# Moving one x step a chunk later, and a set of accumulator loads a few products earlier, in the feed-forward of a hybrid decoder layer

## The reference

```python
x = layer_norm(alpha * x + mix, ln1_g, ln1_b)            # x: (2048, 1024)
ff = jnp.square(jax.nn.relu(x @ w_ff1)) @ w_ff2          # w_ff1: (1024, 4096), w_ff2: (4096, 1024)
x = layer_norm(alpha * x + ff, ln2_g, ln2_b)
```

## Time and profile before

| | before |
|---|---|
| median of 3 runs | 2166.41 us |
| lowest, highest | 2164.86, 2171.97 us |
| the profiled execution's own time | 2171.97 us |
| its span, first to last instruction | 2170.3 us |
| TensorE matmul busy | 2082.6 us, 96% |
| VectorE, ScalarE, GpSimd busy | 64%, 46%, 24% |
| mean granted TensorE clock | 0.987 of full speed |
| DMA, mean over the span | 172 GB/s |

### The profile page before, as it was taken

How to read it: one execution, slowest core, us unless ns; L and a number is a source line. 1 busy time by engine, 2 the same in 40 slices (tenths; PEclk the granted TensorE clock), 3 DMA queues, 4 the chain that set the end, 5 groups by cost and what they waited for, 6 DMA issues and landing times.

```text
span 2170.3 us, 28904 instructions
## 1 busy us (share of the span) xinstructions
PE 2082.6 (96%) x11392; PEld 1685.1 (78%) x11392; DVE 1389.6 (64%) x1898; ACT 1006.3 (46%) x1344; POOL 516.7 (24%) x483
## 2 busy tenths in 40 slices
PE   7999999999999999799999999999999999999996
PEld 5677787778777777688888788888788888788884
DVE  3668566756765687656556776666665645954458
ACT  3535454444444445545445654544433333633334
POOL 3002001101110213011000244444684700810004
PEclk9999999999999999899999999999999999999998
DMA  6222333324242514255646778777968665665563
GB/s 196 59 59 88 107 95 121 107 78 143 72 127 59 175 53 134 87 189 196 221 153 218 270 256 285 248 272 271 333 203 284 196 193 187 222 224 194 193 194 136
DMA packets 241063, 374.26 MB, mean 172 GB/s; under 512 B 16368, under 2 KB 117776, under 8 KB 240928
## 3 DMA queue, kind: packets, MB, share of 16 engines
q1 hardware_dynamic: 212096, 272.68, 38.6%
q0 software_dynamic: 28832, 99.74, 13.3%
HBM read 272.74 MB, written 99.61 MB: 172 GB/s over the span
## 4 chain that ended last, share of the span: by engine, by line
PE 51%; DVE 6%; ACT 2%; DMA 2%; issue 1%; POOL 0%; SPq 0%; DVEq 0%; ACTq 0%; POOLq 0%
PE main L68 9%; PE main L70 9%; PE main L69 9%; PE sc L68 6%; PE sc L69 6%; PE sc L70 6%; DVE w_lo L1563 3%; PE aux L70 1%; PE ob L70 1%; PE ob L68 1%; PE aux L68 1%; PE ob L69 1%; PE aux L69 1%; DMA w_b<-in_w_ff_dram 1%; DMA x_piece<-normed_dram 1%
## 5 line engine op out<-in xcount | busy, mean ns | idle before, releaser
L1563 DVE TENSOR_TENSOR w_lo<-w_b,w_hi 128x1024 fp32r<-128x1024 f32 x144 | 217.5, 1513 | 241.5 <-ACT w_hi L1533 241.5
L1563 DVE TENSOR_TENSOR w_lo<-raw,w_hi 128x1024 fp32r<-128x1024 f32 x144 | 205.5, 1430 | 128.6 <-ACT w_hi L1533 128.6
L1533 ACT ACTIVATE w_hi<-raw 128x1024 fp32r<-128x1024 f32 x144 | 152.5, 1060 | 256.7 <-PE main L70 112.6
L1533 ACT ACTIVATE w_hi<-w_b 128x1024 fp32r<-128x1024 f32 x144 | 152.2, 1057 | 176.9 <-PE aux L70 81.3
L1053 DVE TENSOR_TENSOR w_lo<-raw,w_hi 128x1024 fp32r<-128x1024 f32 x116 | 140.9, 1222 | 140.4 <-ACT w_hi L763 139.6
L68 PE MATMUL main<-xT_lo,w_hi 128*128 128x512 f32 (+1 forms) x528 | 217.2, 411 | 1.5 <-DVE xT_lo L1065 1.5
L69 PE MATMUL main<-xT_hi,w_lo 128*128 128x512 f32 (+1 forms) x528 | 205.5, 389 | 0.0
L70 PE MATMUL main<-xT_hi,w_hi 128*128 128x512 f32 (+1 forms) x528 | 205.4, 389 | 0.0
L68 PE MATMUL sc<-x_lo,w_hi 128*128 128x512 f32 x448 | 175.6, 392 | 8.4 <-DVE x_lo L1506 6.1
L68 PE MATMUL main<-x_lo,w_hi 128*128 128x512 f32 x448 | 175.7, 392 | 8.0 <-ACT z L1884 8.0
L68 PE MATMUL main<-w_lo,w_hi 128*128 128x512 f32 x448 | 175.8, 392 | 5.1 <-DVE w_lo L1563 5.0
(11 more groups left out here) (254 smaller groups left out, 4664.7 us busy)
## 6 DMA issues: line engine op xcount, KB each, us to landing
raw<-in_w_in_dram SPq DMA_DIRECT2D x80, 512.0 KB, 3.7
h_dram<-z SPq DMA_DIRECT2D x64, 512.0 KB, 3.9
raw<-h_dram SPq DMA_DIRECT2D x112, 256.0 KB, 2.7
w_b<-h_dram SPq DMA_DIRECT2D x112, 256.0 KB, 2.7
h_dram<-h_s SPq DMA_DIRECT2D x48, 512.0 KB, 4.0
rows<-in_x_dram POOLq DMA_DIRECT2D x32, 512.0 KB, 4.9
raw<-in_w_out_dram SPq DMA_DIRECT2D x32, 512.0 KB, 3.7
raw<-in_w_ff_dram SPq DMA_DIRECT2D x32, 512.0 KB, 6.7
```

The lines of the kernel that those rows point to most:

```text
L1533: act.activation(ff.w_hi[:, n % RING, :], slot_tile(ff, m), ACT.Copy).then_inc(ff.hi_done, 1)
L1563: dve.tensor_tensor(ff.w_lo[:, n % RING, :], slot_tile(ff, m), ff.w_hi[:, n % RING, :].bitcast(F32), ALU.subtract).then_inc(ff.lo_done, 1)
```

## The change

Two things are done. First, the late x steps are spread otherwise: before, chunk 0 does step 8, chunk 1 steps 9 and 10, chunk 2 steps 11 and 12, and chunks 3, 4 and 5 one each (13, 14, 15). After, chunk 2 does only step 11, after product 4, and chunks 3, 4, 5 and 6 do 12 to 15. Second, GpSimd waits for `EXPAND_SLOTS` instead of three slots more before it loads the rows; the first four `acc` loads wait for slots 1 to 4 instead of 4 to 7; and the other four come ahead of `init`, waiting for slots 6 to 9, instead of being spread between its first four steps and waiting for slots 8 to 11.

```diff
 def x_late_step(chunk):
-    return X_STEPS + chunk + min(chunk, 2)
+    return X_STEPS if chunk == 0 else X_STEPS + 1 + chunk
...
-        pool.wait_ge(slot_used, EXPAND_SLOTS + 3)
+        pool.wait_ge(slot_used, EXPAND_SLOTS)
         load_row(g1_row, ln1_g)
         load_row(b1_row, ln1_b)
         for c in range(4):
-            load_acc(0, c, 4 + c)
+            load_acc(0, c, 1 + c)
         pool.wait_ge(row_landed, 16 * 2)
         for row in (g1_row, b1_row):
             pool.tensor_scalar(row[:, :], row[:, :], ALPHA, None, ALU.mult).then_inc(row_scaled, 1)
+        for c in range(4, 8):
+            load_acc(0, c, 2 + c)
         pool.wait_ge(row_scaled, 2)
 
         def init(hf):
             for i, (c, d) in enumerate(INIT_ORDER):
-                if hf == 0 and i < 4:
-                    load_acc(0, 4 + i, 8 + i)
...
-                if o == 1 and chunk in (1, 2):
-                    x_transposes(pe, ff, x_late_step(chunk) - 1)
-                elif o == 4 and chunk < HALF_CHUNKS - 2:
+                if o == 1 and chunk == 1:
+                    x_transposes(pe, ff, X_STEPS + 1)
+                elif o == 4 and chunk < HALF_CHUNKS - 1:
                     x_transposes(pe, ff, x_late_step(chunk))
```

More of the change, by code:

```diff
@@ L1929, in _ @@
             back(1)
-            if chunk in (1, 2):
-                x_evacuate(act, ff, x_late_step(chunk) - 1)
+            if chunk == 1:
+                x_evacuate(act, ff, X_STEPS + 1)
             snapshot(chunk, 2, a)
@@ L1942, in _ @@
             squared(chunk, 2, z11)
-            if chunk < HALF_CHUNKS - 2:
+            if chunk < HALF_CHUNKS - 1:
                 x_evacuate(act, ff, x_late_step(chunk))
@@ L2038, in _ @@
             low(1)
-            if chunk in (1, 2):
-                x_sums(dve, ff, x_late_step(chunk) - 1)
+            if chunk == 1:
+                x_sums(dve, ff, X_STEPS + 1)
             low(2)
```

## The result

| | before | after |
|---|---|---|
| median | 2166.41 us | 2179.81 us (2175.77 to 2180.07, 5 runs) |
| ratio | | 1.0057, 95% interval 1.0046 to 1.0068 (+12.3 us) |
| profiled execution, its span | 2171.97, 2170.3 | 2182.1, 2180.4 |
| VectorE, ScalarE, GpSimd busy | 64%, 46%, 24% | 63%, 46%, 24% |

The kernel became slower, as forecast (2177.0, range 2167 to 2184). The +12.3 goes by the ratio, which rests on more runs than the medians in the table; these lie 13.4 apart, and 12.3 with the 2167.49 that 29 later runs of before gave. The page after hardly differs: the same instructions, the same bytes, TensorE busy at 96%.

A forecast was written before the change was run, and what follows sets the result against it. TensorE's matmul row, busy 96% of the span, was taken as the bound. Chunk 7's net +8.0 and the second product's +2.6 gave +10.6: 2182.6 for the profiled execution, a median of 2177.0, range 2167 to 2184.

The forecast's parts named there:

- Chunk 2 and chunk 6: Expand part: the step leaving chunk 2 gives back 1.67 us, chunk 6's added step costs 0.93; together -0.7.
- Chunk 7: Reads back land late, the z sums pass 9.6 us on to chunk 8; +8.0 with chunk 2's 1.67 taken off.
- The clock behind chunk 7's waits: After TensorE's gaps around chunk 7: a lowered clock adds up to 1.7 us, a bound only.
- The contract part: Start of the second matrix product: GpSimd's earlier loads push back SyncE's for products 8 to 10; +2.6, bounds -4.5 and +5.5.
- the sum over bytes asked for: Second product's start: 1.0 MB more asked for by 1547, at about 0.39 MB/us, is 2.6 us later.
- reads that land quickly: Rival, chunk 7: reads land in 4.2 us, r2 4.6 late, net 2.9; total 2171.9; chance 0.14.
- a relieved burst: Rival, second product: earlier GpSimd loads clear SyncE's way, 4.5 us come back; total 2169.9; chance 0.14.
- keep its start near 1554: Contract part: `init` was to start near 1554 as before, with the accumulators not waited for.
- the turns between queues: DMA engines alternate between queues with work, so SyncE's loads keep a half share however long GpSimd's queue is.

The follow-up runs named there:

- e1: Only the change's x steps moved, GpSimd's loads as before, against the kernel before: 2175.41 us, ratio 1.0039.
- e3: e1 with chunk 6's x step after product 1 instead of product 4, timed against the kernel before: 2167.12 us, ratio 0.9996.
- e5: e1 with ScalarE's back(0) placed behind the snapshot of product 1 and the w_hi after it, timed against the kernel before: 2175.78 us, ratio 1.0042.
- e2: Only GpSimd's row and accumulator loads earlier, as in the change, against the kernel before: 2170.69 us, ratio 1.0018.
- e4: Kernel before with accumulator loads later (waiting for slots 8 to 11 and 12 to 15), rows as before: 2165.75 us, ratio 0.9991.
- e7: The change's x steps with chunk 6's after product 2, plus e4's loads, against the kernel before: 2165.70 us, ratio 0.9996.
- e6: Kernel before with only the two row loads three slots earlier, accumulator loads unchanged: 2167.58 us, ratio 0.9998.

## Why the prediction was right, step by step

The sign and the size were right (+10.6 forecast, +12.3 measured) and came from the steps named. By term:

- **Chunk 2 and chunk 6**: -1.67 and +0.93 forecast, -1.71 and +0.89 measured. Chunk 2 takes 1028.59 - 989.62 = 38.97 us now.
- **Chunk 7**: 43.3 us forecast from chunk 7's snapshot to chunk 8's first product (1231.8 - 1188.5), 43.39 measured (1227.94 - 1184.55), 34.59 before (in e1 42.73, so the closeness to a tenth is luck). The single steps were off by up to a microsecond and cancelled: r0's read 7.8 us instead of 8.4, r1's and r2's 9.9 instead of 9.3, r5's (issued 1204.45, converted from 1208.74) 4.3 instead of 5.26; the wait for the snapshot was 5.55 instead of 4.4. e3 shows that the reads' lateness is the cause, and e5 that the snapshot's wait is not; that the z sums' loop carries it is read from their unchanged distance of 7.80 us. That the same reads had already been measured in the same company is what made this term good. The rule from the Trainium skill ("DMA: Bandwidth & Descriptors", Anatomy of one DMA), an estimate of 3.2 us, was again less than half of what r0, r1 and r2 took in company.
- **The clock behind chunk 7's waits**: I had it as a bound of up to 1.7 and counted nothing. After the 5.55 us wait the window 1200 to 1204 shows 0.50, which cost nothing, since product 3 still ended before the first z sum could begin for the reads' sake. Behind the wait of 2.08 at chunk 8 the clock fell in the changed kernel (0.65, then 0.92), and the stretch to the end of the expand part is 0.96 longer. But e1 and e5 have the same wait (2.08 and 2.10), their clock stays at 1.00 behind it, and their stretch is as long as before's (305.58, 305.59 and 305.59). So the 0.96 isn't a steady cost of the change, and counting nothing was right as far as single executions can tell. The windows of after and e1:

```profile
1228.00:1232.00 4.00, 4.00 (x12) 3.21 (x13) 3.10 (x3) 3.97 (x5) 0.00 (x0) 0.65 0.88 313
```

```profile
1228.00:1232.00 4.00, 4.00 (x19) 3.31 (x18) 3.10 (x3) 3.65 (x4) 0.65 (x1) 1.00 0.80 303
```

- **The contract part**: +2.6 forecast, +3.4 in the profile of after, +3.9 for e2 in the timed runs. Mis-sized by about one: the waits grew from 2.3 to 4.5 us, and the clock fell twice instead of once in this execution, which stood in the bound only (in e2's profile the waits were 3.8 us and the clock fell once). Where the delay falls was wrong: I had the loads for products 8 to 10 land 2.6 us later, but TensorE waited at products 7 and 8, and product 7's load took 15.0 us instead of 5.7. Before, that load had about 6.3 us to spare: it landed at 1538.1, product 7 began about 1546.8, and the conversion takes 2.4. Counted from the relu it landed 8.9 us later in the changed kernel, so 2.6 were left as a wait. That this equals my 2.6 is luck, since the sum over bytes asked for knows nothing of time to spare. Its direction holds: more bytes ahead of SyncE's loads cost (e2), and fewer take the waits away (e4).
- **The rivals**: reads that land quickly, and a relieved burst, both fell. A relief shows in the profiles when the loads are later, not earlier (e4, e7: no waits). In the timed runs it is -1.7 by the medians, with intervals that reach no change, and less than the 4.5 us that I read from before's profile. That profile was the slowest of before's executions; of the four profiles with the loads as before, two show the fall of the clock in this stretch and two don't.
- `init` didn't keep its start near 1554: its first step came at 1568.09, since the last two `acc` loads waited for slots that were themselves late. Nothing waited for it.

What stays open: how much of the contract part's loss is the wait and how much the clock in a typical execution, since only one of each kernel is profiled; and whether it is the bytes in the DMA engines or SyncE's own long issues (last section) that make the load for product 8 late. No run separates the sum over bytes asked for from the turns between queues that the prediction named beside it.

## What to carry to other kernels

When a hand-placed step is moved later, follow what it releases to the first in-order queue that wants it, and compare the cover (here 37 us) with the shift (39 us, one chunk): for the landing times take the rows of the same transfers in the same company. Where a late input enters a loop that is already slower than the engine it feeds, its lateness is passed on whole, and the largest wait seen on that engine may be only a symptom. In a stretch where the DMA share is about 1.0, a transfer moved earlier is a transfer put ahead of someone; first see who that is, and how long before its use it lands. When a profile shows a loss behind a wait, see whether another kernel's profile with the same wait shows it too, before it is counted as the change's.

## What the runs showed of the hardware that I had not expected

SyncE's issues themselves can grow long while the DMA share is about 1.0. After the change:

```profile
1542.19 4.05 SPq L1631 DMA_DIRECT2D raw<-h_dram  x1
1546.28 1.64 SPq L1641 DMA_DIRECT2D raw<-in_w_ff_dram  x1
```

An issue of line 1631 whose median over the run is 0.32 us took 4.05, and 4.01 at the same place in e2, so the loads queued behind it on SyncE left late as well as landing late; before, the longest of that line was 1.53 us, and with the rows alone earlier (e6) 1.45. The last four stores of the expand part's result took 12.3 to 16.9 us to land, and 5.0 to 6.5 before.

The length of a wait alone doesn't say whether the clock falls behind it. Waits of 1.80 us (before), 1.89 and 2.64 (after) and 2.23 (e2) in the contract part were followed by windows at 0.60 to 0.64, and the 2.08 at chunk 8 in after by 0.65; the 1.99 before and the 2.08 and 2.10 of e1 and e5 at chunk 8 were followed by 1.00.
